# Two neighbouring ring slots per transfer in the weight stream of a two-layer decoder step

## The reference, cut to what matters

```python
for i in range(DEPTH):                      # 2
    hn = _rmsnorm(h, g_mix[i])
    h = h + (mla(hn) if i % 2 == 0 else sgu(hn))
    h = h + _hier_moe(_rmsnorm(h, g_ffn[i]), ...)
    h = h + sigmoid(_rmsnorm(h, g_ple[i]) @ ple_w_gate[i]) * (p[i] @ ple_w_proj[i])
y = _rmsnorm(h, g_final)
# _hier_moe, per expert e: y += (silu(t @ w_gate[e]) * (t @ w_up[e]) * gate[:, e]) @ w_down[e]
```

## Time and profile before

| | |
|---|---|
| median of 3 runs | 1240.37 us (1238.86 to 1242.16) |
| the profiled execution, its time | 1241.1 us |
| its span in the profile | 1239.3 us |
| PE busy | 1081.3 us, 87% |
| DMA, mean over the span | 248 GB/s, 306.80 MB |
| the stream's queue (with the key pages and x) | 275.93 MB, 56.1% of 16 engines' time |

### The profile page before, as it was taken

How to read it: one execution, slowest core, us unless ns; L and a number is a source line. 1 busy time by engine, 2 the same in 40 slices (tenths; PEclk the granted TensorE clock), 3 DMA queues, 4 the chain that set the end, 5 groups by cost and what they waited for, 6 DMA issues and landing times.

```text
span 1239.3 us, 14327 instructions
## 1 busy us (share of the span) xinstructions
PE 1081.3 (87%) x5212; PEld 664.5 (54%) x5212; DVE 363.0 (29%) x897; ACT 193.5 (16%) x396; POOL 112.8 (9%) x150
## 2 busy tenths in 40 slices
PE   5898879899988986579999999999989998887393
PEld 4675546644433332467777777777654443332172
DVE  1243332522222210335223644421242221211254
ACT  2121211311111111112111211000111111111121
POOL 0134100111111100100000000000011111110101
PEclk9998889999999999679999999999989999999787
DMA  9628636289999996843333323333359999999401
GB/s 384 247 76 246 194 111 270 77 339 420 418 419 418 420 420 278 326 178 121 136 132 110 133 102 111 120 132 108 128 195 391 417 417 419 419 420 415 158 38 38
DMA packets 62596, 306.80 MB, mean 248 GB/s; under 512 B 13730, under 2 KB 23170, under 8 KB 30402
## 3 DMA queue, kind: packets, MB, share of 16 engines
q1 hardware_dynamic: 45360, 275.93, 56.1%
q0 software_dynamic: 13632, 22.58, 5.6%
q10 hardware_dynamic: 3538, 7.39, 1.6%
HBM read 308.88 MB, written 21.08 MB: 266 GB/s over the span
## 4 chain that ended last, share of the span: by engine, by line
PE 63%; DMA 25%; DVE 5%; issue 4%; ACT 1%; POOL 0%; SPq 0%; POOLq 0%; ACTq 0%; DVEq 0%
DMA ring_sb<-stream 22%; PE ps L1511 15%; PE ps L1374 10%; PE ps L1559 8%; PE ps L1383 4%; PE ps L1446 3%; PE ps L1293 3%; PE ps L1108 2%; PE ps L1128 2%; PE ps L1334 2%; DMA scr_sb<-y_rows 1%; DMA scr_sb<-bs 1%; PE ps L1325 1%; PE ps L1462 1%; PE ps L1457 1%
## 5 line engine op out<-in xcount | busy, mean ns | idle before, releaser
L1374 PE MATMUL ps<-ring_sb,scr_sb 128*64 128x512 f32 x1024 | 236.9, 609 | 40.5 <-DMA ring_sb<-stream 40.4
L1511 PE MATMUL ps<-hn_sb,ring_sb 128*128 128x288 f32 x768 | 194.9, 408 | 0.0
L1374 PEld LDWEIGHTS ps<-ring_sb,scr_sb 128*64 128x64 f32 x1024 | 79.0, 140 | 193.5 <-issue 193.5
L1511 PEld LDWEIGHTS ps<-hn_sb,ring_sb 128*128 128x128 f32 x768 | 142.6, 190 | 37.3 <-DVE hn_sb L692 0.3
L1383 PE MATMUL ps<-ring_sb,scr_sb 128*64 128x512 f32 x512 | 120.3, 613 | 2.8 <-ACT scr_sb L577 2.8
L1559 PE MATMUL ps<-scr_sb,ring_sb 128*128 128x288 f32 x384 | 95.3, 407 | 0.0
L922 DVE SCALAR_TENSOR_TENSOR scr_sb<-ps,scr_sb 128x256 f32<-128x256 f32 x32 | 15.5, 484 | 266.8 <-ACT scr_sb L573 266.8
L1559 PEld LDWEIGHTS ps<-scr_sb,ring_sb 128*128 128x128 f32 x384 | 72.2, 190 | 19.4
L1446 PE MATMUL ps<-scr_sb,ring_sb 128*128 128x288 f32 x256 | 70.0, 427 | 0.0
L1383 PEld LDWEIGHTS ps<-ring_sb,scr_sb 128*64 128x64 f32 x512 | 34.7, 139 | 62.2 <-issue 57.5
L335 POOL DMA_INDIRECT scr_sb<-hn_rows,scr_sb x32 | 32.4, 1014 | 297.6 <-DVE scr_sb L904 273.8
(11 more groups left out here) (245 smaller groups left out, 1077.1 us busy)
## 6 DMA issues: line engine op xcount, KB each, us to landing
ring_sb<-stream SPq DMA_DIRECT2D x250, 1024.0 KB, 19.7
scr_sb<-key_pages SPq DMA_DIRECT2D x64, 192.0 KB, 3.4
ring_sb<-row_pages POOLq DMA_DIRECT2D x64, 128.0 KB, 3.2
scr_sb<-y_rows POOLq DMA_DIRECT2D x8, 512.0 KB, 5.1
hn_rows<-scr_sb ACTq DMA_DIRECT2D x4, 512.0 KB, 3.2
h_sb<-x SPq DMA_DIRECT2D x1, 1152.0 KB, 5.5
y_out<-hn_sb ACTq DMA_DIRECT2D x8, 144.0 KB, 1.8
scr_sb<-bs ACTq DMA_DIRECT2D x1, 640.0 KB, 13.2
```

Source lines behind the costliest of these rows:

```text
L1374: last = mm(ps[64 * a:64 * a + 64, 2 + b, :], xT[:, k, 64 * a:64 * a + 64], slot(a + 2 * (k // 4))[:, (k % 4) * 512:(k % 4) * 512 + 512], ...
L1511: last = mm(bank((i + 1) % 4, T), ring(s, (i % 2) * D + k * P, P), hn_t[:, k, :], start=(k == 0), stop=(k == KD - 1))
```

## The change

A transfer now carries two neighbouring slots, s and s+1 with s even, and six semaphores, one for each pair of positions, take the place of twelve. `load_slot` becomes `load_two`; it waits until both positions are given back (s - 10 slots free) and copies 128 x 2 x 2048 floats, each partition's two rows of 8 KB from two places 1 MB apart. PE waits for the pair's semaphore whichever of the two slots it needs. PE still gives back slots one by one. The wait for `y12_in2` now stands before the transfers (110, 111) and (248, 249). The stream, its order and all computation are as before.

```diff
         for s in range(s0, s1):
             pos, n = slot_pos(s)
-            pe.wait_ge(sem(f"slot_full{pos}"), 16 * n)
+            pe.wait_ge(sem(f"slot_full{pos // 2}"), 16 * n)
...
-        def load_slot(s):
+        def load_two(s):
             pos, _ = slot_pos(s)
             if s >= RING:
-                sp.wait_ge(sem("slot_free"), s - RING + 1)
-            sp.dma_start(ring(pos, 0, SLOT), stream[s]).then_inc(sem(f"slot_full{pos}"), 16)
+                sp.wait_ge(sem("slot_free"), s - RING + 2)
+            sp.dma_start(ring(pos, 0, 2 * SLOT).rearrange("p (s n) -> p s n", s=2),
+                         stream[s:s + 2].rearrange("s p n -> p s n")).then_inc(sem(f"slot_full{pos // 2}"), 16)
...
             with sp.Fori(r0, r1) as i:
-                for j in range(RING):
-                    sp.wait_ge(sem("slot_free"), i * RING + (j + 1 - RING))
-                    sp.dma_start(ring(j, 0, SLOT), stream[bass.ds(i * RING + j, 1)].rearrange("a p n -> (a p) n")
-                                 ).then_inc(sem(f"slot_full{j}"), 16)
+                for j in range(0, RING, 2):
+                    sp.wait_ge(sem("slot_free"), i * RING + (j + 2 - RING))
+                    sp.dma_start(ring(j, 0, 2 * SLOT).rearrange("p (s n) -> p s n", s=2),
+                                 stream[bass.ds(i * RING + j, 2)].rearrange("s p n -> p s n")
+                                 ).then_inc(sem(f"slot_full{j // 2}"), 16)
...
-        for s in range(S_SGU // RING * RING, S_SGU // RING * RING + RING):
-            if s == S_GATE[0] + 2:
+        for s in range(S_SGU // RING * RING, S_SGU // RING * RING + RING, 2):
+            if s in (S_GATE[0] + 1, S_GATE[0] + 2):
                 sp.wait_ge(sem("y12_in2"), 32)
-            load_slot(s)
+            load_two(s)
```

More of the change, by code:

```diff
@@ L288, in _ @@
         sp.dma_start(h_t[:, :, :], io["x"]).then_inc(sem("x_in"), 16)
-        for s in range(RING):
-            load_slot(s)
+        for s in range(0, RING, 2):
+            load_two(s)
         sp.wait_ge(sem("ptab_in"), 16)
@@ L297, in _ @@
         sp.wait_ge(sem("rows_free"), 8)
-        for s in range(RING, 2 * RING):
-            load_slot(s)
+        for s in range(RING, 2 * RING, 2):
+            load_two(s)
         def load_rounds(r0, r1):
             with sp.Fori(r0, r1) as i:
-                for j in range(RING):
-                    sp.wait_ge(sem("slot_free"), i * RING + (j + 1 - RING))
-                    sp.dma_start(ring(j, 0, SLOT), stream[bass.ds(i * RING + j, 1)].rearrange("a p n -> (a p) n")
-                                 ).then_inc(sem(f"slot_full{j}"), 16)
+                for j in range(0, RING, 2):
[3 more added lines that the diff above has]
+                                 ).then_inc(sem(f"slot_full{j // 2}"), 16)
         load_rounds(2, S_SGU // RING)
-        for s in range(S_SGU // RING * RING, S_SGU // RING * RING + RING):
-            if s == S_GATE[0] + 2:
+        for s in range(S_SGU // RING * RING, S_SGU // RING * RING + RING, 2):
+            if s in (S_GATE[0] + 1, S_GATE[0] + 2):
                 sp.wait_ge(sem("y12_in2"), 32)
-            load_slot(s)
+            load_two(s)
         load_rounds(S_SGU // RING + 1, S_GATE[1] // RING)
-        for s in range(S_GATE[1] // RING * RING, N_SLOTS):
-            if s == S_GATE[1] + 2:
+        for s in range(S_GATE[1] // RING * RING, N_SLOTS, 2):
+            if s in (S_GATE[1] + 1, S_GATE[1] + 2):
                 sp.wait_ge(sem("y12_in2"), 64)
-            load_slot(s)
+            load_two(s)
     @block.gpsimd
```

## The result

With a transfer for every two slots the kernel takes 1244.93 us (median of 20 runs, 1236.71 to 1256.05); before it took 1240.13 (20 runs, 1234.66 to 1243.75). The ratio is 1.0042, 95% interval [1.0025, 1.0059]: slower by some 5 us. The slowest run, 1256.05, is left out of the ratio as a disturbed one. The prediction said 1246.7.

What follows compares the result with a forecast made beforehand. The DMA stream was taken to bound both MoE stages at 2.70 us a slot. 2.7 + 2.7 + 1.2 + 0.6 - 0.9 = 6.3 us on the 1240.37 median gave 1246.7 us; forecast 1243.9 to 1250, range 1240.7 to 1252.

Steps and rivals of the forecast that it cites:

- What bounds the kernel: Both MoE stages: the end is when the queue last stood empty plus remaining slots times 2.70 us, not PE's pace.
- 1, start of the first stage: First MoE stage's start: slot 24 waits for 25's release, so one slot more passes before the end, +2.7 us.
- 2, end of the first stage: First MoE stage's end: PE's last second half also waits for slot 107, one slot time later, +2.7 us.
- 3, second stage: Second MoE stage: slot 166 waits for 167's release while the queue runs out, +1.2 us; nothing at the end.
- The 0 for the down product: Second MoE stage's end: both slots land 5.4 us behind the half's, within its distance of 5.84, so 0 added.
- 4, start of the kernel: Kernel start: PE's first product with weights now also waits for slot 3, +0.6 us.
- 5, cost of a transfer: Both MoE stages: pairs save half a small packet per slot and engine, -0.9 us over about 160 slots.
- 6, other places: Slot 110, the bs load, slots 12 to 23, gated-unit stages and SP: 0, with bs bounds 0 and +2.7 us.
- The rival of slower cases: Whole kernel: slower packets, to 1264 us, or bs one slot later plus a clock dip, 1250 to 1254; chance 0.12.
- Larger transfers: Both MoE stages: a per-transfer cost saved once for every two slots makes the kernel faster, 1233 or 1240 us; chance 0.10.
- The lost slots: First MoE stage's start and end: lost slots are hidden, 3.7 us or less remains, about 1243; chance 0.16.
- The pitch of 1 MB: Both MoE stages: packets alternating between places 1 MB apart take 4% longer, 17 us, to 1264; within a 0.12 chance.

Runs made afterwards that it cites:

- the release by two alone: Kernel before, single transfers and waits, but an even slot is issued only when its odd neighbour's place is free too: 1240.63 us, ratio 1.0012.
- waiting for both: Kernel before, single transfers and releases, but PE waits until both slots of a pair have landed: 1242.92 us, ratio 1.0023.
- the kernel with rows spread: Kernel before, with each expert's gathered token rows permuted to other partitions: 1223.72 us, ratio 0.9876.
- both edits: Kernel before, still 250 one-slot transfers, but PE waits for both slots of a pair and they are issued only when both places are free: 1244.29 us, ratio 1.0043.

## Why the prediction was right

**What bounds the kernel: right.** Both stages end when the stream has passed, at 419 GB/s in either form, and PE's last second half waits 1.28 and 1.25 us for it. The time lies in the lower half of the forecast's own range, 1243.9 to 1250. By the runs the sum is 0.6 at the start, 3.6 in the first stage, some 0.5 in the second and 0.3 at its end, 5.0 us, and a lower clock in some places.

**1, start of the first stage: right in mechanism, a little large.** Slot 24 does go with 25, 4.68 us after the first product, to the tenth of a us. Slots 26 and 27 have landed 18.34 us after the first product, where 27 used to land 15.79 after it: 2.55 later, nearly a slot time. The term was 2.7; the release by two alone costs 2.3 to 2.5 at the end of the stage.

**2, end of the first stage: right in mechanism, mis-sized.** The term was a full slot time, 2.7; waiting for both costs 1.5 to 1.7. In the kernel with rows spread, where the engines land close together, both terms come out at 4.5 together with the saving, near the full 4.95. The 2.7 assumed that slot 107 lands one slot time after 106 on the engine that is last; the trace of before has 485.26 - 482.17 = 3.1 there. But slot 107 did not land at the same time in the run with the wait: it was there 232.81 us after the first product (at 480.76), and in the two profiles of before 234.40 and 234.18 after it. By these traces the waiting itself moved it. GpSimd's scatter of a finished pair follows PE's work (it is issued at 478.02, 4.3 us ahead of the last second half; with the wait at 476.65, again 4.3 ahead), and PE's work now stands one landing later in the stream. So in the last 3.09 us before slot 107 is there, q0, the indirect queue, moves 0.13 MB in the kernel before (first pair of rows, 482.17 to 485.26) and 0.02 MB with the wait (second pair, 477.67 to 480.76), and the stream moves more:

```profile
q1 hardware_dynamic: 85, 0.61, 47.1%
q0 software_dynamic: 96, 0.13, 11.2%
```

```profile
q1 hardware_dynamic: 106, 0.77, 59.3%
q0 software_dynamic: 63, 0.02, 2.8%
```

The prediction held the stream fixed while PE's wait moved. That the later scatter gives back all of the 1.4 to 1.6 us is read from these traces and was not tested by a run.

**3, second stage: right.** 166 waits for 167's release, as in the rows above. 166 and 167 have landed 25.78 and 26.51 us after the first product in the two profiles, where 167 used to land 24.83 and 25.05 after it, about 1 us earlier. The stage is longer by 0.1 to 0.9 us; 1.2 less its part of the saving, 0.8, was forecast, and two profiles of the kernel before differ by as much. The 0 for the down product was wrong by 0.3: both its slots land together, 6.14 us after the half's start instead of 5.84. The point put 5.4 us under 5.84, two slot times of 2.70; but the engine that lands last is slower than the mean: its part of slot 245 came 6.13 us behind that of 243 in the kernel before (1148.82 and 1154.95).

**4, start of the kernel: right.** The first weight product is at 19.66 and 19.75; 19.5 was forecast. Slots 2 and 3 had landed at 19.41 and 19.50. But the kernel before had it at 18.88 and at 19.25 in its second profile, so 0.4 to 0.9 us is the change, and single profiles vary by 0.4.

**5, cost of a transfer: right, small.** 0.9 us saved was forecast in both stages. The stage of layer 0 shows 0.6 for single transfers against pairs, on its own 84 slots. Packets of the stream's queue in 300 to 480, beside the 9828 of the earlier trace rows:

```profile
q1 hardware_dynamic: 9292, 71.60, 95.6%
q0 software_dynamic: 3174, 3.47, 5.5%
```

536 packets fewer at the same share of the engines' time: the small packets are worth next to nothing. In the trace of before one took 9.3 ns in the mean (11 in the prediction), a row of 8 KB 314 ns.

**6, other places: right.** The wait for bs is 7.76 us (7.99 before) and the product behind it comes 4.03 later, less than the 4.33 of the last second half: nothing was lost there.

**Not in the sum.** The lower clock in the last down product of layer 1, 1.7 us in the profiles that show it. It is in both profiles of the changed kernel and in neither of the kernel before, but also in the one with both edits and in the one with the release alone. From the last second half to PE's first product behind the pair (L1459, L1457 before) it is 28.83 and 29.18 us in the changed kernel; the kernel before has 25.88 in one profile and 27.50 in the other, so a single pair of profiles can't say what the change adds there. The rival of slower cases named a clock dip, without a place. Against the 4.8 us of the medians the forecast of 6.3 was 1.5 too large, and 1.0 to 1.2 of that is term 2.

**The rivals.** Larger transfers are not faster to speak of: single transfers with both edits are as slow as pairs (1.0043 against 1.0046), and four slots are slower still. The Trainium skill, DMA: Bandwidth & Descriptors, section Bandwidth, has throughput grow with a transfer's size; where transfers queue, this case's windows do not agree: 1 and 2 MB both flow at 419 GB/s, and 4 MB at 397 to 409. The lost slots were not hidden; 3.5 to 3.7 of the 4.95 us in the first stage were paid. The pitch of 1 MB between a packet and the next costs nothing that the windows show.

## What to carry to other kernels

Where a stream sets the end of a stage, count in slots: how many pass between the moment when the queue last stood dry and the landing that the last consumer waits for; a coarser transfer adds slots at both ends. The one at the end goes away if transfers begin where the consumer's need begins, but padding that does this can put more slots behind the last release ahead of the stage, as in layer 1 here. A landing later in the stream also moves other traffic that follows the consumer, so a slot can cost less than a slot time. In this kernel 1 MB transfers that queue back to back had 0.6 us in a stage to win from being 2 MB, and a ring of twelve slots cut into three transfers starved its own queue. Before making transfers larger, look at how far apart the engines' parts of one transfer land: here that was worth three times what the change cost.

## What the hardware showed that was not expected

The parts of one 1 MB slot landed over 15.7 us in the kernel before (466.5 to 482.2; over 15.5 us in its second profile), six slot times, though the mean share of the engines is full and the page shows nothing of it. It was small at the start of the stage (slot 24: 255.15 to 255.57) and grew with it. Moving the gathered rows to other partitions cut it to 5.7 us and the kernel by 1.2% (ratio 0.9876 [0.9849, 0.9903]), with the same bytes, the same count of packets and the same 419 GB/s. And a pair issued at 256.34 to a queue that had all but run dry had landed only at 264.24, 7.9 us later with the pair before it just done, where single slots 25 and 26 issued at 255.54 and 256.14 had landed at 260.39 and 262.92: whatever part of a pair is there earlier, PE can't use it before the whole has come.
